# Weight buffers and moving tensors at different offsets modulo 512 bytes

## The reference

```python
def block_fn(args):                      # the experts, per block of tokens
    xb, eb, gb = args
    a = jnp.einsum('cd,ced->ce', xb, u_tab[eb]).astype(jnp.float32)
    w = (gb * jax.nn.gelu(a, approximate=False)).astype(xb.dtype)
    return jnp.einsum('ce,ced->cd', w, v_tab[eb])
...
for l in range(DEPTH_2):                 # the second block's layers
    h = _rms_norm(x, attn_norm[l])
    proj = h @ w_in[l]
    ...
    x = x + mixed @ w_out[l]
    h = _rms_norm(x, mlp_norm[l])
    x = x + jnp.square(jax.nn.relu(h @ w_ff1[l])) @ w_ff2[l]
return _rms_norm(x, final_norm)
```

## Time and profile before

| what | value |
|---|---|
| time, two runs | 1676.55 and 1690.06 us, median 1683.3 us |
| profiled execution, first to last instruction | 1675.2 us |
| TensorE busy | 1601.4 us, 96% |
| weight loads busy | 1462.2 us, 87% |
| GpSimd / ScalarE / VectorE busy | 1196.0 / 925.5 / 883.8 us |
| read from memory | 277.30 MB, 166 GB/s over the span |
| mean granted clock of TensorE | 0.991 |

### The profile page before, as it was taken

One profiled execution on the slowest core, in us unless ns is written; L12 is line 12 of the kernel. 1 busy time (PEld: TensorE's weight loads), 2 busy tenths in 40 slices (PEclk: granted clock), 3 DMA queues, 4 the chain that ended last, 5 costly groups with the idle time before them and its releaser, 6 DMA issues.

```text
span 1675.2 us, 32062 instructions
## 1 busy us (share of the span) xinstructions
PE 1601.4 (96%) x12800; PEld 1462.2 (87%) x12800; DVE 883.8 (53%) x1817; ACT 925.5 (55%) x1553; POOL 1196.0 (71%) x500
## 2 busy tenths in 40 slices
PE   7988999999999999999999999998999998989997
PEld 7876999999999998888888888768999996789997
DVE  6988445994366667777511115876220068752101
ACT  6666655445444445555566656565653457656533
POOL 5552777998877777787888887215888861268885
PEclk9999999999999999999999999999999999999999
DMA  7441555666655555555666664513566645146663
GB/s 256 131 134 39 180 174 176 193 197 189 189 177 174 175 174 172 176 174 171 195 196 191 189 191 143 194 51 117 185 190 195 194 152 176 51 131 197 191 197 116
DMA packets 79891, 280.42 MB, mean 167 GB/s; under 512 B 8704, under 2 KB 9472, under 8 KB 79488
## 3 DMA queue, kind: packets, MB, share of 16 engines
q1 hardware_dynamic: 79744, 278.38, 53.4%
HBM read 277.30 MB, written 1.05 MB: 166 GB/s over the span
## 4 chain that ended last, share of the span: by engine, by line
PE 83%; DVE 6%; issue 4%; ACT 4%; POOL 2%; DMA 0%; POOLq 0%; DVEq 0%; SPq 0%; ACTq 0%
PE ps L2661 14%; PE ps L2029 13%; PE ps L2330 10%; PE ps L2639 7%; PE ps L2668 7%; PE ps L2640 7%; PE ps L2644 7%; PE ps L538 6%; POOL wl L199 2%; ACT wh L184 1%; PE ps L2625 1%; PE ps L2627 1%; PE ps L372 1%; PE ps L2153 1%; PE ps L2087 1%
## 5 line engine op out<-in xcount | busy, mean ns | idle before, releaser
L199 POOL TENSOR_TENSOR wl<-slots,wh 128x1024 fp32r<-128x1024 f32 x236 | 571.5, 2425 | 339.5 <-ACT wh L184 315.5
L2439 POOL TENSOR_TENSOR wl<-slots,wh 128x1024 fp32r<-128x1024 f32 x256 | 619.7, 2423 | 124.5 <-ACT wh L2377 122.4
L2377 ACT ACTIVATE wh<-slots 128x1024 fp32r<-128x1024 f32 x256 | 271.9, 1062 | 351.1 <-issue 229.0
L184 ACT ACTIVATE wh<-slots 128x1024 fp32r<-128x1024 f32 x236 | 249.7, 1060 | 240.3 <-PE ps L2330 98.9
L2639 PE MATMUL ps<-xh,wh 128*128 128x256 f32 x1024 | 241.9, 279 | 0.0
L2640 PE MATMUL ps<-xl,wh 128*128 128x256 f32 x1024 | 238.9, 276 | 0.0
L2639 PEld LDWEIGHTS ps<-xh,wh 128*128 128x128 f32 x1024 | 192.4, 188 | 0.1
L2640 PEld LDWEIGHTS ps<-xl,wh 128*128 128x128 f32 x1024 | 192.4, 188 | 0.0
L2661 PE MATMUL ps<-wh,xh 128*128 128x512 f32 x508 | 160.4, 397 | 0.0
L2661 PE MATMUL ps<-wh,xl 128*128 128x512 f32 x508 | 158.0, 392 | 0.0
L2538 DVE TENSOR_TENSOR small<-ps,small 128x512 f16<-128x512 f32 x128 | 87.7, 685 | 108.2 <-PE ps L2627 108.2
(11 more groups left out here) (386 smaller groups left out, 3041.8 us busy)
## 6 DMA issues: line engine op xcount, KB each, us to landing
slots<-w SPq DMA_DIRECT2D x260, 512.0 KB, 3.5
slots<-wu SPq DMA_DIRECT2D x128, 512.0 KB, 3.5
slots<-wv SPq DMA_DIRECT2D x128, 512.0 KB, 3.5
arena<-bias SPq DMA_DIRECT2D x1, 2048.0 KB, 8.1
h<-xT SPq DMA_DIRECT2D x4, 256.0 KB, 7.0
arena<-keys SPq DMA_DIRECT2D x1, 1024.0 KB, 8.6
yT<-y_out SPq DMA_DIRECT2D x2, 512.0 KB, 2.7
layer<-consts SPq DMA_DIRECT2D x1, 800.0 KB, 5.3
```

What stands on the lines that cost most here:

```text
L184: act.activation(self.hi[:, n % 2, :], self.slots[:, u % SLOTS, :], ACT.Copy).then_inc(self.rounded, 1)
L199: pool.tensor_tensor(self.lo[:, n % 2, :], self.slots[:, self.order[n] % SLOTS, :], self.hi[:, n % 2, :].bitcast(F32), ALU.subtract).then_ ...
L2377: act.activation(whv[:, r % 2, :], slots_v[:, r % SLOTS, :], ACT.Copy).then_inc(w_hi, 1)
L2439: pool.tensor_tensor(wlv[:, r % 2, :], slots_v[:, r % SLOTS, :], whv[:, r % 2, :].bitcast(F32), ALU.subtract).then_inc(w_lo, 1)
```

## The change

Only places in memory change. Every buffer of `wh` and `wl` gets 32 spare words (128 bytes) behind it; spare tensors stand above `xh` (112 words) and `xl` (120), and in front of `mix_hi` (32), `mix_lo` (48), `hidden_hi` (56) and `hidden_lo` (8); `below_arena` goes. In the attention part of the second block the tensors from word 9984 on move up by 80 words (320 bytes). The instructions, their order and their waits are the same on every engine.

Distances, moving tensor less stationary tensor, modulo 512 bytes, from the addresses of the two programs:

| moving by stationary | before | after, buffer 0 / 1 |
|---|---|---|
| `xh` by `wh` | 448 | 0 / 384 |
| `xl` by `wh` | 448 | 32 / 416 |
| `xh` by `wl` | 448 | 256 / 128 |
| `early_hi`, `early_lo` by `wh` | 448 | 32 / 416 |
| `early_hi` by `wl` | 448 | 288 / 160 |
| `mix_hi` by `wh` | 448 | 160 / 32 |
| `mix_lo` by `wh` | 448 | 352 / 224 |
| `mix_hi` by `wl` | 448 | 416 / 288 |
| `mix_lo` by `wl` | 448 | 96 / 480 |
| `hidden_hi` by `wh` | 448 | 64 / 448 |
| `hidden_lo` by `wh` | 448 | 96 / 480 |
| `hidden_hi` by `wl` | 448 | 320 / 192 |
| `wh` by `xh` (512 columns) | 64 | 0 / 128 |
| `wh` by `xl` | 64 | 480 / 96 |
| `wl` by `xh` | 64 | 256 / 384 |
| `wh` and `wl` by `row0_hi`, `row0_lo` | 480 | 480 and 224 (row 0 has buffer 0) |

Matmuls in fp32r with 256 columns: 8592 at 448 and 144 at 64 before; after, 1072 at 0, 1208 at 32, 256 at 64, 296 at 96, 1072 at 128, 128 at 160, 256 at 192, 96 at 224, 1072 at 256, 112 at 288, 256 at 320, 96 at 352, 1072 at 384, 1192 at 416, 256 at 448 and 296 at 480. With 512 columns: 1524 at 64 and 12 at 480 before.

```diff
-        xh, xl = (ctx.enter_context(nc.sbuf_tensor(n, [P, DC * T], F32R, side="right")) for n in ("xh", "xl"))
-        wh, wl = sb("wh", 2 * SLOT, F32R), sb("wl", 2 * SLOT, F32R)
+        def right(name, cols):
+            return ctx.enter_context(nc.sbuf_tensor(name, [P, cols], F32R, side="right"))
+
+        right("above_xh", 112)
+        xh = right("xh", DC * T)
+        right("above_xl", 120)
+        xl = right("xl", DC * T)
+        wh = sb("wh", 2 * (SLOT + 32), F32R)
+        wl = sb("wl", 2 * (SLOT + 32), F32R)
...
-        sb("below_arena", 104)
...
-        whv, wlv = (x[:, :].rearrange("p (b n) -> p b n", b=2) for x in (wh, wl))
+        whv, wlv = (x[:, :].rearrange("p (b n) -> p b n", b=2)[:, :, 0:SLOT] for x in (wh, wl))
...
-        mix_hi, mix_lo, hidden_hi, hidden_lo = (
-            sb(n, chunks * T, F32R)[:, :].rearrange("p (c t) -> p c t", t=T)
-            for n, chunks in (("mix_hi", 8), ("mix_lo", 8), ("hidden_hi", FC), ("hidden_lo", FC)))
+        def spaced(name, words, chunks):
+            sb("below_" + name, words)
+            return sb(name, chunks * T, F32R)[:, :].rearrange("p (c t) -> p c t", t=T)
+
+        mix_hi = spaced("mix_hi", 32, 8)
+        mix_lo = spaced("mix_lo", 48, 8)
+        hidden_hi = spaced("hidden_hi", 56, FC)
+        hidden_lo = spaced("hidden_lo", 8, FC)
...
         def lpart(a, b):
-            return low_part[:, a:b] if b <= 5888 else attention[:, a - 5888:b - 5888]
+            if b <= 5888:
+                return low_part[:, a:b]
+            shift = 80 if a >= 9984 else 0
+            return attention[:, a - 5888 + shift:b - 5888 + shift]
```

## The result

The changed kernel takes 1713.4 us (1713.33 and 1713.51) where the kernel before takes 1683.3 us in the median of its two runs: a ratio of 1.0175, interval 1.0139 to 1.021. The profiled spans are 1711.7 and 1675.2 us, 36.5 us apart. The interval reaches over 2%, so these runs leave open on which side of 2% the change lies. In the three later series before took 1677 to 1680 us; against that the change costs 34 to 36 us, though the changed kernel was not timed in those series.

A forecast was written before the change was run, and what follows sets the result against it. TensorE was taken as the bound, through the start-to-start pace of its fp32r matmuls. Terms of 15.6 + 3 us, rounded down to 18, gave 1693 us profiled and 1701 us on the median; range 1670 to 1755 us.

The forecast's parts named there:

- within 2%: Whole kernel: change of at most 34 us, taking in the mixed-levels forecast, no effect and a part of the edges.
- Term (a): 256-column fp32r matmuls: half of those moved stand at 117.8 ns instead of 9 in 100, costing 15.6 us.
- the high level: 256-column fp32r matmuls: the slower of two paces, 117.8 ns start to start against 113.3, both seen at distance 448.
- Term (b): 512-column fp32r matmuls: half of them go from 229 to 233 ns, costing 3 us.
- The sign read at row 0: Down projection: ten matmuls of row 0 at distance 480 took 233 ns each, against 229 in row 1.
- Terms (c) and (d): Plain fp32 and fp16 matmuls, and ScalarE's rounding and GpSimd's subtraction at new addresses: all costed at nothing.
- No effect: Rival for all matmuls: addresses don't make load and stream disturb each other, timing alone makes the levels; 1683 us, chance 0.25.
- the rule that loading weights takes nothing from the running matmul: TensorE: two independent read ports, so distance can't matter and the time stays 1683 us.
- Near distances colliding: Rival at distances 0, 32 and 480: 22 ns more on 3088 matmuls, 68 us, 1751 us; chance 0.18.
- The stall going away: Rival for moved matmuls: half reach 108.4 or 217 ns, gaining 30 us; three in four, 45 us, 1638 us; chance 0.08.
- GpSimd as the bound of the scan: Rival in the expert scan: subtraction 15% slower (2787 ns), at most 33 us over the program, 1716 us; chance 0.04.
- All at the high level: Rival: every distance but 448 and 64 stands at the slower pace, 41 us, 1724 us; chance 0.10.

The follow-up runs named there:

- D 56: Weight views begun inside their tensors against the kernel before, so that moving less stationary is 56 bytes for all 256-column matmuls: 1711.3 us, ratio 1.0204.
- D 0: Spare words (112) ahead of the weight buffers of the kernel before, so that moving less stationary is 0 for 256-column matmuls: 1718.9 us, ratio 1.025.
- D 32, 48, 80 and 96: Four runs, weights alone moved against the kernel before, one 256-column distance each (32, 48, 80, 96 bytes): 1706.6, 1705.6, 1713.1 and 1728.4 us.
- D 0 and 256: Two runs, weights alone moved against the kernel before, one 256-column distance each (0 or 256 bytes): 1718.9 and 1718.4 us.
- D 32: Spare words (104) ahead of the weight buffers of the kernel before, so that moving less stationary is 32 for 256-column matmuls: 1706.6 us, ratio 1.0181.

## Why the prediction came out as it did

**The direction and the range held, and "within 2%" in the median**, but that only because one of the two runs of before was slow: the interval of the ratio reaches 1.021, and against the later series of before (1677 to 1680 us) the change costs 2.0 to 2.2%. On the profile's own terms the forecast was 1675.2 + 18 = 1693 us, and the span is 1711.7: the sum was half of what it should be.

**Term (a), half of the 256-column matmuls at the high level, is the one mis-sized.** Forecast 15.6 us. The mean of these intervals went from 113.9 to 118.1 ns, 4.2 x 8736 = 37 us of TensorE's time. The step that failed is "I take it that at the other distances half of the matmuls stand at the high level": the mean at each of the sixteen distances of the changed kernel is 116.6 ns or more, 448 itself included. The premise under it, that 113.3 and 117.8 are all the prices there are, failed as well: one distance alone gives 117.0, 119.3 or 119.9. Averaged over the changed kernel, they happen to lie by the high level (118.1 against 117.8). That the forecast stayed within its range is thus luck in part.

**Term (b)** was 3 us, from a price of 4 ns read on ten matmuls. All 1524 rose by 3.1 ns (229.2 to 232.2), 4.7 us, and the stage got 4.6 us longer. The sign read at row 0 was real: distance 480 alone gives 233.2 ns, as the ten matmuls said. They would have given about the whole term (6 us), had I not halved it. But that size fits by luck in part: in the changed kernel the matmuls at 480 read 230.0 ns, the lowest of the six distances there, and the others 231.9 to 233.4. And row 0 did not move whole: its eight matmuls with `wh` keep 480.

**Terms (c) and (d)**, nothing, held: 386 and 384 ns at other distances, and 2416 for 2423 ns on GpSimd, 1062 for 1062 on ScalarE. That no place could touch GpSimd would have been wrong: 2007 ns at D 56.

**What the sum leaves out.** Not all of a longer matmul reaches the end: 37 + 4.7 = 42 us of stretched intervals made 36.5 us of span. The runs with one distance agree (D 0: 6.0 x 8736 - 1.7 x 1524 = 50 us, and 42 us measured). The two traces hold the same matmuls in the same order and can be laid beside each other. The intervals without a wait in either differ by 40.1 us: 5.5 in the mixers, 12.9 in the up scan, 4.7 in the down scan, 8.6 and 8.4 in the two layers. Against that, the intervals of fp32r matmuls with a wait got 5.8 us shorter, 3.4 of it in the mixers and 1.0 and 0.9 in the layers. There TensorE waits for another engine that was not slowed, and when it comes later it finds less to wait for. The mixers' costliest group shows it, before and after:

```profile
L538 PE MATMUL ps<-xh,wh 128*128 128x256 f32 x368 | 56.3, 297 | 15.8 <-ACT xh L652 8.7 <-DVE arena L959 3.3 <-ACT wh L184 1.7
```

```profile
L544 PE MATMUL ps<-xh,wh 128*128 128x256 f32 x368 | 57.6, 300 | 14.1 <-ACT xh L658 7.4 <-DVE arena L965 2.9 <-ACT wh L184 1.6
```

The last 2.5 us, the other way, lie between other matmuls of the mixers, and have no cause shown.

**The rivals.** No effect is refuted by every run with one distance other than 64 modulo 128, and with it what I drew from the rule that loading weights takes nothing from the running matmul (the Trainium skill, TensorE: Matmul & The Clock Gate, Step-by-step: what each phase is for), that no placement could change the time. Here placement alone makes 42 us at D 0. The granted clock is that of before (0.994 for 0.991), and the load lasts 188 ns at D 32, 48, 80 and 96 and 191 at D 0 and 256, so a longer load doesn't explain it. Whether the load takes reads from the stream after all, or the two meet elsewhere, no run shows. The 109.2 and 215.8 ns that the prediction set beside the trace are, on that page, the gap of a matmul by itself and not of a stream of loads and matmuls, so they are a weak yardstick for it. Near distances colliding was wrong as put: D 32 is among the cheaper ones and 256 as dear as 0, and the dearest 256-column price found is 6 ns, not 22. The stall going away did not happen at any D; the best pace found for 256 columns is the one that the kernel had. For 512 columns 227.5 ns exists, 1.7 ns under it. GpSimd as the bound of the scan did not happen either: its subtraction took 2458 ns in the mean at most, in the run moved by 32 bytes, and a row has 2720. All at the high level (41 us, 1724 us) was priced nearest: 36.5 us. I gave it 0.10 for want of a row at any third distance. No row of before would have made it the forecast. In the up scan and the two longest feed-forward stretches the stream is at the low level throughout, which could be read as the sign of a special place; but the run moved by 32 bytes has the feed-forward stretches all at the high level at the same distance, so that sign is weak.

## What to carry to other kernels

In a dense stream of fp32r matmuls with a weight load each, the distance between the two operands is worth up to 6% of the pace at 256 columns, where it looks periodic in 128 bytes; hold it at one value for neighbouring matmuls, here 64, and measure that value for each shape, since the best one for 512 columns was another (0). When placement is not controlled, a spare tensor or a resized buffer can move a kernel by 2 to 3% with no instruction changed, so compare paces and not only times before crediting an edit. And when a kernel has two levels for the same work, look which one each run stood at: here a step of 12 us between runs of one program can be just that. A weight buffer that starts 8 bytes off is worth a try where a GpSimd subtraction like this one is the bound: it was 17% faster in the one run that had it.

## What the runs showed of the hardware that was not expected

Start to start, fp32r with 256 columns: 113.3 ns at 64 modulo 128 (with a second level of 117.8 that is there from a wait on and was seen to last through 1376 matmuls), 117.0 at 32 and 119.9 at 96 as means of intervals that go round in fours and sixes, and 120 at 0 and 256, within 1 ns in 8012 of 8512 and 8007 of 8518 intervals. 8 bytes beside 64 cost 5.4 ns in the mean, 16 bytes 3.0 and 4.3, the weights' start off a multiple of 32 bytes included. fp32r with 512 columns: 227.5 ns at 0 and 256, 229 to 230 at 64, 232 to 235 at 480, 464, 456, 432 and 416. Plain fp32 matmuls show none of this at the distances that occur; the fp16 ones kept theirs in every run, so they were not tested. GpSimd's subtraction of 128 x 1024 elements: 2007 ns with `wh` and `wl` starting 8 bytes off a multiple of 16, 2411 to 2452 in all other runs (a profile's times on GpSimd are rough, but all 492 of them moved together, 1196.0 to 994.8 us in sum). What stays open: the mechanism itself (what the two reads share, and what picks the level at a wait), whether 8 and 16 bytes beside 64 cost by the distance or by the start of the weights, 128 and 384 as the only distance of a kernel (their likeness to 0 is inferred from 256), and a version that keeps 64 for 256 columns and 0 for 512, worth 1.7 x 1524 = 3 us by these paces, which was not tried. No version tried beats the kernel before.
